# A two-block transformer kernel: the loads of shift and scale in eight 1 MB pieces, x's chunks ahead of the context's, and the low parts multiplied last

## The chip, the cores and the metric

The kernel runs on one core of one Trainium2 chip. The metric is the device time of one execution in microseconds (us). Three runs of the kernel before gave 1496.94 us in the median (1495.87 to 1498.08).

## The reference, cut to what matters

The program computes two transformer blocks on 512 tokens of 1024 features, all in float32. Only the very start of the first block is touched:

```
mod_l = split(silu(c) @ ada_w + ada_b, 6)          # ada_w: 1024 x 6144; shift, scale, gate, ...
mod_c = split(silu(c_ctx) @ ada_w + ada_b, 6)
h  = rmsnorm(x)   * norm1_g * (1 + scale)   + shift      # 512 tokens
hc = rmsnorm(ctx) * norm1_g * (1 + scale_c) + shift_c    # 256 tokens
z  = h @ w_in;   v = z[..., 1024:1536]
kvc = hc @ w_in[:, 512:1536]                             # its second half gives the context's v
```

Behind it stand the attention, the gating, the convolution and the feed-forward part of the first block, and the whole second block.

## The kernel before, in words

The program is written engine by engine: each engine has its own hand-written order of instructions, and semaphores tie them together. An engine's order is strict, so whatever waits holds up everything behind it on that engine. Features lie on the 128 partitions in eight chunks k = 0 to 7, and tokens along the free dimension.

**Products.** Every large product runs as three float32r matmuls: low times high, high times low, high times high. Of each weight tile ScalarE (ACT) makes the high part (`prepare`, L1092) and VectorE (DVE) the low part (`low`, L1547). Tiles arrive by SyncE (SP) in three raw slots, and three split tiles are kept.

**The beginning** runs until the first product of the tile called g0. It holds:

- The tiles of shift and scale, `ada_turned`: 16 tiles of 512 KB in seven slots, which are borrowed from buffers that are used later (`v_mid`, `q_loc`, `sg_out`, `sg_v`, `v_ctx`, `probs_more`). On PE, `modulation(i)` (L601) multiplies one with silu(c) and silu(c_ctx). Four tiles make a quarter. DVE copies the quarter's sums (L1635), PE adds up its parts (`selected`, L613), and DVE makes shift and gain for two chunks (`gains_of`, L1641 and L1644).
- The two norms: ACT squares (L1099), DVE adds (L1564), PE sums over partitions (`norm_sum`, L559), ACT takes the root (L1104), DVE its reciprocal (L1568), PE spreads it (`norm_spread`, L573), ACT copies it out (L1142 for x, L1154 for the context), and DVE multiplies (L1650, L1660).
- The chunks: ACT writes `exact` and then `h_hi` (`modulated`, L1119 and L1121), or `normed` and then `hc_hi` (`context`, L1128 and L1130). DVE subtracts for the low part (`modulated_lo`, L1655, and `context_lo`, L1665).
- The products for v: `own(k)` is 12 matmuls for chunk k of x (four token tiles into banks 0 to 3), `context(k)` is 6 for chunk k of the context (banks 4 and 5). Weight tile t holds chunks 2t and 2t + 1. So `own(4)` and `context(4)` need the third tile, and `own(6)` the fourth.
- Eight rows of `ada_rows` for the later gates: `early_rows` on DVE (L1573), in the same seven slots.

PE's order is: tile 0, sums of x's norm, tile 1, spread, tiles 2 and 3, selection 0, `own(0)`, tiles 4 to 7, selection 1, `own(1)`, `own(2)`, sums of the context's norm, tiles 8 to 11, `own(3)`, spread, selection 2, `context(0)`, `context(1)`, `own(4)`, tiles 12 to 15, `own(5)`, selection 3, `context(2)`, `context(3)`, `own(6)`, `context(4)`, `context(5)`, `own(7)`, `context(6)`, `context(7)`. Then g0 starts.

## Time and profile before

| | |
|---|---|
| median of three runs | 1496.94 us |
| the profiled execution | 1495.27 us |
| its span in the profile | 1494.0 us |
| PE busy | 1421.7 us, 95% of the span |
| DVE, ACT busy | 51%, 41% |
| start of the first product of g0 | 80.97 us |
| PE busy before 81.00 us | 57.89 us |

Times in the trace count from the span's start. A row of a timeline is a run of equal instructions: where it starts, how long it took, engine, line, operation, what it writes and reads, and, in brackets, how long the engine had been idle and what ended that. A row of the table by stage gives the busy time of each engine, the granted clock of PE as a share of full speed, the share of time in which the DMA engines were busy, and GB/s.

### The profile page before, as it was taken

To read this page: it belongs to the slowest core of one execution; us is meant where nothing else is said; L and a number is where in the kernel's file an instruction comes from. 1 tells how busy PE (TensorE), PEld (TensorE's weight loads), DVE (VectorE), ACT (ScalarE), POOL (GpSimd) and SP (SyncE) were. 2 spreads that over 40 slices of the span, in tenths; PEclk is the share of its full clock that TensorE was granted. 3 is DMA by queue.
4 is the path that set the end of the run, shared out by engine and by line. 5 is a ranking of instruction groups with operands and counts; after the bars stand their busy time and mean duration, and the time that the engine had idled before them with its cause. 6 is when DMAs were issued, how large, how long until landed. Compare 5 with 4: busy or idle time off the path is not lost.

```text
span 1494.0 us, 16901 instructions
## 1 busy us (share of the span) xinstructions
PE 1421.7 (95%) x6826; PEld 1147.6 (77%) x6826; DVE 766.4 (51%) x1005; ACT 617.6 (41%) x856; POOL 14.3 (1%) x20
## 2 busy tenths in 40 slices
PE   5899998989999999999999999999969999999997
PEld 3677776778888888887878877888857888888886
DVE  3568865555554443335327763443266566564224
ACT  4546776363333332223337643322334343343221
POOL 0000000000000000000000000000010000000000
PEclk9999999999999999999999999999959999999999
DMA  8653321303433233331321112233202323223331
GB/s 331 236 162 134 125 74 55 136 29 127 164 132 98 86 95 90 92 104 43 113 85 38 34 43 78 92 99 113 85 15 100 98 85 101 96 85 103 94 100 57
DMA packets 44317, 150.43 MB, mean 101 GB/s; under 512 B 4944, under 2 KB 7120, under 8 KB 44112
## 3 DMA queue, kind: packets, MB, share of 16 engines
q1 hardware_dynamic: 43360, 144.76, 29.3%
q0 software_dynamic: 880, 4.59, 1.0%
q8 instruction: 55, 0.90, 0.2%
q14 instruction: 22, 0.18, 0.0%
HBM read 146.45 MB, written 2.10 MB: 99 GB/s over the span
## 4 chain that ended last, share of the span: by engine, by line
PE 75%; DVE 3%; ACT 1%; issue 1%; POOL 0%; DVEq 0%; ACTq 0%
PE banks L514 23%; PE banks L516 23%; PE banks L515 23%; PE banks L932 1%; PE banks L933 1%; PE banks L559 1%; PE banks L927 1%; PE banks L966 1%; PE banks L924 1%; PE banks L963 1%; PE banks L573 0%; DVE y_buf L2117 0%; DVE x_res L2121 0%; DVE x_res L2056 0%; DVE y_buf L2052 0%
## 5 line engine op out<-in xcount | busy, mean ns | idle before, releaser
L514 PE MATMUL banks<-h_lo,w_hi 128*128 128x512 f32 x1184 | 475.1, 401 | 15.8 <-DVE cv_acc L1836 3.7
L1547 DVE TENSOR_TENSOR w_lo<-raw_w,w_hi 128x1024 fp32r<-128x1024 f32 (+2 forms) x229 | 266.2, 1164 | 402.6 <-ACT w_hi L1092 402.2
L516 PE MATMUL banks<-h_hi,w_hi 128*128 128x512 f32 x1184 | 469.8, 397 | 0.0
L515 PE MATMUL banks<-h_hi,w_lo 128*128 128x512 f32 x1184 | 469.7, 397 | 0.0
L1092 ACT ACTIVATE w_hi<-raw_w 128x1024 fp32r<-128x1024 f32 (+2 forms) x229 | 230.0, 1006 | 285.0 <-PE banks L516 263.3
L514 PEld LDWEIGHTS banks<-h_lo,w_hi 128*128 128x128 f32 x1184 | 224.8, 190 | 74.1 <-issue 20.5
L516 PEld LDWEIGHTS banks<-h_hi,w_hi 128*128 128x128 f32 x1184 | 224.5, 190 | 53.0
L515 PEld LDWEIGHTS banks<-h_hi,w_lo 128*128 128x128 f32 x1184 | 224.8, 190 | 50.1
L516 PE MATMUL banks<-a_hi,w_hi 128*128 128x512 f32 (+1 forms) x374 | 142.5, 381 | 0.0
L515 PE MATMUL banks<-a_hi,w_lo 128*128 128x512 f32 (+1 forms) x374 | 142.2, 380 | 0.0
L514 PE MATMUL banks<-a_lo,w_hi 128*128 128x512 f32 (+1 forms) x374 | 141.7, 379 | 0.0
L515 PEld LDWEIGHTS banks<-a_hi,w_lo 128*128 128x128 f32 x374 | 70.3, 188 | 14.8
L514 PEld LDWEIGHTS banks<-a_lo,w_hi 128*128 128x128 f32 x374 | 70.3, 188 | 14.5
L516 PEld LDWEIGHTS banks<-a_hi,w_hi 128*128 128x128 f32 x374 | 70.3, 188 | 13.7
L1616 DVE SCALAR_TENSOR_TENSOR exact<-banks,cols_sb,exact 128x510 f32<-128x510 f32 (+1 forms) x44 | 33.0, 750 | 53.5 <-ACT exact L1507 52.7
L1616 DVE SCALAR_TENSOR_TENSOR normed<-banks,cols_sb,normed 128x510 f32<-128x510 f32 (+1 forms) x66 | 49.2, 746 | 5.2 <-ACT normed L1507 2.9
L1507 ACT ACTIVATE exact<-banks,cols_sb 128x512 f32<-128x512 f32 x22 | 15.1, 688 | 83.1 <-PE banks L516 83.1
L1107 ACT ACTIVATE a_hi<-normed 128x512 fp32r<-128x512 f32 x44 | 27.8, 633 | 48.7 <-DVE normed L1894 32.0
L1610 DVE SCALAR_TENSOR_TENSOR cv_acc<-cv_in,cols_sb,cv_acc 128x512 f32<-128x512 f32 x60 | 45.0, 749 | 1.4
L1789 DVE SCALAR_TENSOR_TENSOR x_res<-banks,mod,x_res 128x512 f32<-128x512 f32 x22 | 16.2, 749 | 45.1 <-PE banks L516 45.1
L1350 ACT ACTIVATE normed<-normed 128x512 f32<-128x512 f32 x22 | 13.9, 632 | 53.0 <-DVE normed L1890 53.0
L514 PE MATMUL banks<-w_lo,h_hi 128*128 128x512 f32 x64 | 27.1, 423 | 4.7 <-DVE h_lo L1655 3.0
(291 smaller groups left out, 1549.1 us busy)
## 6 DMA issues: line engine op xcount, KB each, us to landing
raw_w<-in_w_ffn_up SPq DMA_DIRECT2D x44, 512.0 KB, 3.4
raw_w<-in_w_up SPq DMA_DIRECT2D x44, 512.0 KB, 3.4
raw_w<-in_ada_rows SPq DMA_DIRECT2D x24, 512.0 KB, 4.0
raw_w<-in_w_gates SPq DMA_DIRECT2D x16, 512.0 KB, 3.2
raw_w<-in_w_ffn_down SPq DMA_DIRECT2D x16, 448.0 KB, 3.3
raw_w<-in_w_down SPq DMA_DIRECT2D x16, 448.0 KB, 3.3
raw_w<-in_w_conv SPq DMA_DIRECT2D x12, 512.0 KB, 3.2
raw_w<-in_w_out SPq DMA_DIRECT2D x10, 512.0 KB, 3.3
```

The source lines that it names most:

```text
L514: e.matmul(dst, lhs_hi, rhs_lo, start=first, stop=False)
L515: e.matmul(dst, lhs_lo, rhs_hi, start=False, stop=False)
L516: return e.matmul(dst, lhs_hi, rhs_hi, start=False, stop=last)
L559: done = e.matmul(bank[b][:, t:t + 1], part[:, t * P:(t + 1) * P], ones[:, :], start=(first and t == 0), stop=(last and t == nt - 1), skip ...
L924: done = e.matmul(bank[0][:, DIAG[j]], keys, q2[part, c, j * P:(j + 1) * P], start=True, stop=True)
L1092: e.activation(w_hi[:, t % KEPT, 0:n], raw[:, i % RAW, 0:n], ACT.Copy).then_inc(s_hi, 1)
L1107: e.activation(dst, src, ACT.Copy).then_inc(done, 1)
L1507: e.activation(dst, bank[b[n]][:, :], ACT.Copy, scale=col("conv_ffn_w_2", w)).then_inc(s_up2_centre.sem, 1)
L1547: e.tensor_tensor(w_lo[:, s, 0:n], raw[:, i % RAW, 0:n], w_hi[:, s, 0:n].bitcast(F32), ALU.subtract).then_inc(s_lo, 1)
L1610: e.scalar_tensor_tensor(out=acc, in0=src, scalar=col("cv_w", i), in1=acc, op0=ALU.mult, op1=ALU.add).then_inc(s_tap_v, 1)
L1616: return e.scalar_tensor_tensor(out=y[:, shift:T], in0=src[:, 0:T - shift], scalar=w, in1=y[:, shift:T], op0=ALU.mult, op1=ALU.add)
L1789: e.scalar_tensor_tensor(out=x[:, o, :], in0=bank[b][:, :], scalar=mod[:, gate + o:gate + o + 1], in1=x[:, o, :], op0=ALU.mult, op1=ALU.ad ...
```

## The change

**Loads of shift and scale.** The same 8 MB come as 8 tiles of 1 MB in a buffer of their own with six slots (`EARLY_SLOTS`). `modulation(i)` now multiplies one such tile, with 8 matmuls where it had 4, and two tiles make a quarter. The eight rows of `ada_rows` come as four transfers of 1 MB in the slots 2, 3, 0 and 1. The buffer lies over `q_loc`, `v_mid`, `v_ctx`, `sg_out`, `sg_v`, `cv_in`, `sg_small` and `hc_hi`, so that their first writers wait: `hc_hi` for the sixth tile's product, the zeros beside `cv_in` (now on DVE behind the last early row) and the load of `sg_small` (now behind that of `v_mid`) for the eight rows.

**SP's queue.** All four transfers of x come first, then `consts` and `cols`, and tile 0 behind them.

**The norm of x.** DVE adds the eighth square too, so that PE sums once (4 instructions for 8). PE does that ahead of tile 0.

**Low parts last.** `values_of` multiplies the high part of a chunk with both parts of the weights, and only then waits for the chunk's low part. ACT writes the high part ahead of `exact` and `normed`.

**Orders.** PE takes `own(4)` ahead of `context(0)`, and `context(4)` ahead of `own(6)`. ACT and DVE follow in orders of their own.

```diff
-EARLY = 7
-ADA_TILES = 16
+EARLY_SLOTS = (0, 1, 2, 3, 4, 5, 0, 1, 2, 3, 0, 1)
+ADA_TILES = 8
...
-        n_one, n_ctx, n_two = NormSems(0), NormSems(0), NormSems(0, add=0, sum=KC)
+        n_one, n_ctx, n_two = NormSems(0, add=KC - 1), NormSems(0), NormSems(0, add=0, sum=KC)
...
+        def early_at(i):
+
+            slot = EARLY_SLOTS[i]
+            return early[:, slot, :, :], (s_early[slot], 16 * EARLY_SLOTS[:i + 1].count(slot))
...
-                e.wait_ge(*ready.at(k + 1))
+                e.wait_ge(*n_hi.at(k + 1))
                 for n, b in enumerate(banks):
                     if k == 0:
                         free(b)
                     tok = slice(n * P, (n + 1) * P)
-                    done = product(bank[b][:, :], src_hi[:, k, tok], src_lo[:, k, tok], hi[:, w], lo[:, w], k == 0, k == KC - 1)
...
+                    e.matmul(bank[b][:, :], src_hi[:, k, tok], lo[:, w], start=(k == 0), stop=False)
+                    e.matmul(bank[b][:, :], src_hi[:, k, tok], hi[:, w], start=False, stop=False)
+                e.wait_ge(*n_lo.at(k + 1))
+                for n, b in enumerate(banks):
+                    tok = slice(n * P, (n + 1) * P)
+                    done = e.matmul(bank[b][:, :], src_lo[:, k, tok], hi[:, w], start=False, stop=(k == KC - 1))
...
+            e.wait_ge(s_ones, 1)
+            e.wait_ge(*n_one.add.at(KC - 1))
+            sum_over_partitions(n_one.bank, exact[:, 0, :], TT, True, True).then_inc(n_one.sum.sem, 1)
             e.wait_ge(s_silu_c, 1)
             modulation(0)
-            norm_sum(n_one, exact[:, 0, :], squares[:, 0, :], TT)
-            modulation(1)
             norm_spread(n_one, TT)
             freed[n_one.bank] = (s_factor, 1)
+            modulation(1)
+            selected(0)
+            own(0)
             modulation(2)
             modulation(3)
-            selected(0)
-            own(0)
-            for i in range(4, 8):
-                modulation(i)
+            own(1)
             selected(1)
-            own(1)
             own(2)
             norm_sum(n_ctx, k_ctx[:, 0, :], squares[:, 0, 0:CTX], CT)
-            for i in range(8, 12):
-                modulation(i)
+            modulation(4)
             own(3)
+            modulation(5)
             norm_spread(n_ctx, CT)
             freed[n_ctx.bank] = (s_factor_ctx, 1)
             selected(2)
+            own(4)
             context(0)
+            own(5)
             context(1)
-            own(4)
-            for i in range(12, 16):
-                modulation(i)
-            own(5)
+            modulation(6)
+            modulation(7)
+            context(2)
             selected(3)
-            for k in range(2, KC):
-                context(k)
-                if k in (3, 5):
-                    own((k + 9) // 2)
+            context(3)
+            context(4)
+            own(6)
+            context(5)
+            own(7)
+            context(6)
+            context(7)
...
             e.dma_start(silu_c[:, :, :], io["c_cols"]).then_inc(s_c, 16)
-            load_x(0)
-            load_x(1)
+            for i in range(KC // 2):
+                load_x(i)
             e.dma_start(consts[:, :], io["consts"]).then_inc(s_consts, 16)
-            load_x(2)
-            load_x(3)
-            load_early(0, 2)
             e.dma_start(cols[:, :], io["cols"]).then_inc(s_cols, 16)
-            load_early(2, 4)
+            load_early(0, 1)
             load(0, 1)
-            load_early(4, 8)
+            load_early(1, 4)
             load(1, 2)
             e.dma_start(xc[:, :, :], io["ctx"]).then_inc(s_xc, 16)
-            load_early(8, 12)
+            load_early(4, 6)
+            load(2, 3)
+            load_early(6, ADA_TILES)
```

The order of the instructions shows what became of the calls. Three places matter. The line numbers of the change are those of its own file: L638, L639 and L643 are the three matmuls that are L514 to L516 before, L610 is a tile of shift and scale, L1111 the split of the weights, L1138 and L1140 `modulated`, L1148 and L1150 `context`.

PE, from the spread of the context's norm on (`hc_hi` is a chunk of the context, `h_hi` one of x). Before:

```order
L573 MATMUL banks<-consts_sb,rstd 128x128 x2
L613 MATMUL banks<-consts_sb,cv_scratch 128x4 x2
L514 MATMUL banks<-w_lo,hc_hi 128x512
L515 MATMUL banks<-w_hi,hc_lo 128x512
L516 MATMUL banks<-w_hi,hc_hi 128x512
L514 MATMUL banks<-w_lo,hc_hi 128x512
```

In the change:

```order
L579 MATMUL banks<-consts_sb,rstd 128x128 x2
L622 MATMUL banks<-consts_sb,cv_scratch 128x4 x2
L638 MATMUL banks<-w_lo,h_hi 128x512
L639 MATMUL banks<-w_hi,h_hi 128x512
L638 MATMUL banks<-w_lo,h_hi 128x512
L639 MATMUL banks<-w_hi,h_hi 128x512
```

Behind the selection PE now takes chunk 4 of x, which reads the third weight tile, where it took chunk 0 of the context, which reads the first.

ACT, around the split of the third weight tile (`w_hi<-raw_w`; `sg_square` is the factor of the context's norm, `v_loc` holds chunks 4 to 7 of x). Before:

```order
L1154 ACTIVATE sg_square<-banks 128x256
L1128 ACTIVATE normed<-xc,mods,gains 128x256
L1130 ACTIVATE hc_hi<-xc,mods,gains 128x256
L1128 ACTIVATE normed<-xc,mods,gains 128x256
L1130 ACTIVATE hc_hi<-xc,mods,gains 128x256
L1092 ACTIVATE w_hi<-raw_w 128x1024
```

In the change:

```order
L1123 ACTIVATE std<-banks,cols_sb 128x2
L1138 ACTIVATE h_hi<-v_loc,mods,gains 128x8x8x8
L1140 ACTIVATE exact<-v_loc,mods,gains 128x512
L1177 ACTIVATE sg_square<-banks 128x256
L1148 ACTIVATE hc_hi<-xc,mods,gains 128x256
L1150 ACTIVATE normed<-xc,mods,gains 128x256
L1111 ACTIVATE w_hi<-raw_w 128x1024
L1138 ACTIVATE h_hi<-v_loc,mods,gains 128x8x8x8
```

Chunk 4 of x has moved ahead of the norm's factor. The split stands behind chunk 0 of the context where it stood behind chunks 0 and 1, and chunk 4 of x, which is multiplied with this tile, stands ahead of it. On DVE the low part of the tile (`low(3)`) follows in both.

ACT, around the split of the fourth weight tile, from the silu of c's row on. Before:

```order
L1163 ACTIVATE silu_row<-silu_row 128x1024
L1119 ACTIVATE exact<-v_loc,mods,gains 128x512
L1121 ACTIVATE h_hi<-v_loc,mods,gains 128x8x8x8
L1092 ACTIVATE w_hi<-raw_w 128x1024
L1128 ACTIVATE normed<-xc,mods,gains 128x256
L1130 ACTIVATE hc_hi<-xc,mods,gains 128x256
L1128 ACTIVATE normed<-xc,mods,gains 128x256
L1130 ACTIVATE hc_hi<-xc,mods,gains 128x256
L1119 ACTIVATE exact<-v_loc,mods,gains 128x512
```

In the change:

```order
L1186 ACTIVATE silu_row<-silu_row 128x1024
L1148 ACTIVATE hc_hi<-xc,mods,gains 128x256
L1150 ACTIVATE normed<-xc,mods,gains 128x256
L1148 ACTIVATE hc_hi<-xc,mods,gains 128x256
L1150 ACTIVATE normed<-xc,mods,gains 128x256
L1138 ACTIVATE h_hi<-v_loc,mods,gains 128x8x8x8
L1140 ACTIVATE exact<-v_loc,mods,gains 128x512
L1111 ACTIVATE w_hi<-raw_w 128x1024
L1138 ACTIVATE h_hi<-v_loc,mods,gains 128x8x8x8
```

Two chunks of the context (`hc_hi`, `normed`) have moved ahead of chunk 6 of x and of the tile's split.

## Rows read from the trace of the kernel before

**Rows 1.** The page: engines' shares, and the chain that ended last.

```profile
PE 1421.7 (95%) x6826; PEld 1147.6 (77%) x6826; DVE 766.4 (51%) x1005; ACT 617.6 (41%) x856; POOL 14.3 (1%) x20
...
PE 75%; DVE 3%; ACT 1%; issue 1%; POOL 0%; DVEq 0%; ACTq 0%
```

**Rows 2.** PE's timeline up to the first products.

```profile
12.72 1.03 PE L601 MATMUL banks<-v_mid,silu_c 128*2 128x256 f32 x8 [12.72 <-DMA v_mid<-in_ada_turned]
...
15.42 1.85 PE L559 MATMUL banks<-ones,squares 128*128 128x1 f32 x8
...
18.16 2.08 PE L573 MATMUL banks<-consts_sb,rstd 128*128 128x128 f32 x8
...
22.69 0.58 PE L613 MATMUL banks<-consts_sb,cv_scratch 128*128 128x4 f32 x4 [0.64 <-DVE cv_scratch L1635]
26.29 0.77 PE L514 MATMUL banks<-w_lo,h_hi 128*128 128x512 f32 x1 [3.02 <-DVE h_lo L1655]
```

**Rows 3.** PE's timeline inside the first products.

```profile
26.86 0.63 PE L515 MATMUL banks<-w_hi,h_lo 128*128 128x512 f32 x1
27.28 0.63 PE L516 MATMUL banks<-w_hi,h_hi 128*128 128x512 f32 x1
...
29.63 0.39 PE L516 MATMUL banks<-w_hi,h_hi 128*128 128x512 f32 x1
29.86 0.39 PE L514 MATMUL banks<-w_lo,h_hi 128*128 128x512 f32 x1
```

**Rows 4.** PE's timeline: own(2), sums, selections, then restarts, then g0.

```profile
36.75 0.47 PE L514 MATMUL banks<-w_lo,h_hi 128*128 128x512 f32 x1
...
41.15 0.58 PE L559 MATMUL banks<-ones,k_ctx 128*128 128x1 f32 x4 [1.36 <-DVE k_ctx L1564]
...
48.86 0.51 PE L613 MATMUL banks<-consts_sb,cv_scratch 128*128 128x4 f32 x4
52.07 0.47 PE L514 MATMUL banks<-w_lo,hc_hi 128*128 128x512 f32 x1 [2.71 <-issue]
...
64.11 0.50 PE L613 MATMUL banks<-consts_sb,cv_scratch 128*128 128x4 f32 x4
...
69.03 0.50 PE L514 MATMUL banks<-w_lo,h_hi 128*128 128x512 f32 x1 [1.52 <-DVE w_lo L1547]
...
80.97 0.40 PE L514 MATMUL banks<-h_lo,w_hi 128*128 128x512 f32 x1
```

**Rows 5.** By stage: engines busy, granted clock, DMA's share, GB/s.

```profile
12.70:26.20 13.50, 9.90 (x60) 6.43 (x60) 4.32 (x10) 5.68 (x9) 0.00 (x0) 0.99 1.03 419
...
49.40:52.10 2.70, 0.03 (x1) 0.06 (x1) 1.42 (x5) 2.21 (x6) 0.00 (x0) 1.00 1.02 410
53.10:56.40 3.30, 3.30 (x10) 2.55 (x9) 3.00 (x5) 3.30 (x6) 0.00 (x0) 0.52 0.09 34
```

**Rows 6.** ACT's timeline: x's squares, a chunk of x, a weight split, the context's.

```profile
10.05 1.15 ACT L1099 ACTIVATE squares<-x_res 128x512 f32<-128x512 f32 x2 [2.29 <-DMA x_res<-in_x]
...
65.16 0.82 ACT L1119 ACTIVATE exact<-v_loc,mods,gains 128x512 f32<-128x512 f32 x1 [5.04 <-issue]
...
66.59 1.04 ACT L1092 ACTIVATE w_hi<-raw_w 128x1024 fp32r<-128x1024 f32 x1
67.54 0.58 ACT L1128 ACTIVATE normed<-xc,mods,gains 128x256 f32<-128x256 f32 x1
68.03 0.59 ACT L1130 ACTIVATE hc_hi<-xc,mods,gains 128x256 fp32r<-128x256 f32 x1
```

**Rows 7.** DVE's timeline: the norm's adds, the gains, low parts.

```profile
10.71 2.29 DVE L1564 TENSOR_TENSOR exact<-exact,squares 128x512 f32<-128x512 f32 x3 [2.00 <-ACT squares L1099]
...
64.91 0.16 DVE L1644 SCALAR_TENSOR_TENSOR gains<-mods,cols_sb 128x4 f32<-128x4 f32 x1
...
67.15 0.69 DVE L1655 TENSOR_TENSOR h_lo<-exact,h_hi 128x512 fp32r<-128x512 f32 x1
67.75 1.22 DVE L1547 TENSOR_TENSOR w_lo<-raw_w,w_hi 128x1024 fp32r<-128x1024 f32 x1
```

More of the change, by code:

```diff
@@ L297, in two_blocks @@
                 group_factor = sb(mixer, "group_factor", [P, CC * TT * 2])
+                with ExitStack() as beginning:
+                    early = sb(beginning, "early", [P, 6, 2, SLOT])
+                q_loc = sb(mixer, "q_loc", [P, AC, T])
+                v_mid = sb(mixer, "v_mid", [P, CBLK - 1, ATT])
+                v_ctx = sb(mixer, "v_ctx", [P, CT, ATT])
+                sg_out = sb(mixer, "sg_out", [P, SC, T])
+                sg_v = sb(mixer, "sg_v", [P, TT, SG])
+                cv_in = sb(mixer, "cv_in", [P, CC, T + 2 * PAD])
+                sg_small = sb(mixer, "sg_small_sb", [P, SC * P + 2 * SG + 4 * P])
+                hc_hi = sb(mixer, "hc_hi", [P, KC, CTX], F32R)
+                hc_lo = sb(mixer, "hc_lo", [P, KC, CTX], F32R)
                 with ExitStack() as context:
@@ L381, in two_blocks @@
         s_bias = [semaphore(f"in_bias{i}") for i in range(2)]
-        s_early = [semaphore(f"in_early{i}") for i in range(EARLY)]
+        s_early = [semaphore(f"in_early{i}") for i in range(6)]
         s_x = [semaphore(f"in_x{i}") for i in range(KC // 2)]
@@ L593, in modulation @@
             def modulation(i):
-                quarter, m = i // 4, i % 4
+                quarter = i // 2
                 b = ADA_BANKS[quarter]
-                if m == 0:
+                tiles, there = early_at(i)
+                if i % 2 == 0:
                     free(b)
-                e.wait_ge(s_early[i % EARLY], 16 * (i // EARLY + 1))
-                for part in range(4):
-                    done = e.matmul(bank[b][32 * part:32 * part + 2, 0:2 * P], silu_c[:, 2 * m + part // 2, :],
-                                    early[i % EARLY][:, part * 2 * P:(part + 1) * 2 * P], start=(m == 0), stop=(m == 3))
+                e.wait_ge(*there)
+                for half in range(2):
+                    m = 2 * (i % 2) + half
+                    for part in range(4):
+                        done = e.matmul(bank[b][32 * part:32 * part + 2, 0:2 * P], silu_c[:, 2 * m + part // 2, :],
+                                        tiles[:, half, part * 2 * P:(part + 1) * 2 * P], start=(m == 0), stop=(m == 3))
                 done.then_inc(s_modulation, 1)
-                if m == 3:
+                if i % 2:
                     freed[b] = (s_ada_sums, quarter + 1)
@@ L616, in selected, with values_of @@
                 freed[select_bank] = (s_mods, quarter + 1)
[L618 removed]
+            def values_of(k, banks, src, n_hi, n_lo):
+                src_hi, src_lo = src
                 t = W["v"] + k // 2
@@ L1579, in early_rows @@
                 for _ in range(count):
-                    i = ADA_TILES + rows_done
-                    e.wait_ge(s_early[i % EARLY], 16 * (i // EARLY + 1))
-                    row(early[i % EARLY])
+                    tiles, there = early_at(ADA_TILES + rows_done // 2)
+                    e.wait_ge(*there)
+                    row(tiles[:, rows_done % 2, :])
             def rows(before):
@@ L1668, in vector_program @@
                 e.memset(bank[b][:, 0:2 * P], 0.0).then_inc(s_cleared, 1)
-            for k in range(1, KC - 1):
+            for k in range(1, KC):
                 add(n_one, k, exact[:, 0, :], squares[:, (k - 1) % 2, :])
             reciprocal_root(n_one, TT)
+            low(1)
             normed_x(0)
+            modulation(0)
             normed_x(1)
-            modulation(0)
             gains_of(0)
-            low(1)
             modulated_lo(0)
@@ L1707, in vector_program @@
             context_lo(3)
-            early_rows(1)
             normed_context(4)
             normed_context(5)
+            context_lo(4)
+            context_lo(5)
             modulated_lo(6)
             low(4)
-            early_rows(1)
-            context_lo(4)
-            context_lo(5)
-            modulated_lo(7)
-            early_rows(1)
             normed_context(6)
             normed_context(7)
-            early_rows(1)
-            low(W["g0"] + 1)
+            modulated_lo(7)
+            early_rows(2)
             context_lo(6)
             context_lo(7)
+            low(W["g0"] + 1)
+            early_rows(1)
             low(W["g0"] + 2)
-            early_rows(EARLY_ROWS - 4)
+            early_rows(EARLY_ROWS - 3)
+            e.wait_ge(s_row, EARLY_ROWS)
+            for s in (slice(0, PAD), slice(PAD + T, T + 2 * PAD)):
+                e.memset(cv_in[:, :, s], 0.0).then_inc(s_pads, 1)
             def softmax(i):
```

94 lines of the change are left out of this document (44 added, 50 removed).

## The prediction

> **What bounds the kernel now.** I read the page first: PE is busy for 95% of the span and holds 75% of the chain that ended last, far ahead of any other engine [rows 1]. So a microsecond won or lost on PE in the beginning arrives at the end undiminished, as long as PE finds no gap behind g0 to hide it in. Next I read PE's timeline of the beginning, which is all that the change touches. It shows where PE stands still: 12.7 us until tile 0, 3.0 us before `own(0)`, 1.4 us before the sums of the context's norm, 2.7 us before `context(0)`, 1.5 us before `own(6)`, which waits for the low part of the fourth weight tile [rows 2, 4]. g0 starts at 80.97 us, and that start is the number to forecast. The table by stage shows that DMA is saturated early on, at 419 GB/s with a share of 1.03 [rows 5], but of PE's waits only the first one ends on a DMA. The others end on chains through ACT and DVE. So the question is how these chains are ordered.
>
> Prices for PE. A matmul of 512 columns starts every 0.42 us at the lower level of the clock (1.2 GHz) and every 0.23 us at the upper (2.4 GHz) [rows 3]. So a chunk of x (12) costs 5.1 or 2.8 us, a chunk of the context (6) 2.5 or 1.4 us. A tile of 512 KB costs 0.97 us at the lower level (its row's 1.03 less the overlap) [rows 2], about half of that at the upper. The eight sums of 1.85 us and the spread of 2.08 us [rows 2] fell at the lower level too: four sums later took 0.58 us [rows 4].
>
> **Step 1, the lead.** x's third transfer was there at 10.05 us [rows 6]. The 322 KB of constants no longer stand ahead of it, which at 419 GB/s [rows 5] is 0.8 us. The last three adds ended at 13.0 us (10.71 + 2.29) [rows 7]; now they end at 12.2, and one add more (0.6) makes 12.8. One group of sums follows where two were, to 14.7 us. Tile 0 is 1 MB. The queue's bytes up to its end are 3.7 MB where they were 3.0 MB at 12.72 us, so it lands at about 14.5 us, hidden under the sums. It runs to 16.6 (2 x 0.97). The root's table load now stands behind the wait for the sums and is hidden under tile 0. The spread ends at 18.7, ACT's copy and DVE's product for chunk 0 at 20.0. Tile 1 runs 18.7 to 20.6, and DVE's copy lets the selection start at 21.1, where it was 22.69 [rows 2]. From the start of a selection to the end of the gains it takes 0.96 us (64.11 to 65.07) [rows 4, 7], and `h_hi` is written first now and takes 0.8 us, as a chunk's first write does [rows 6]. `own(0)` starts at 23.05 instead of 26.29 us: **a lead of 3.2 us**. The low part is ready long before PE wants it.
>
> **Step 2, it shrinks.** `own(0)` ends at 27.2 (7 matmuls at the lower level, 5 at the upper). Tiles 2 and 3 (1.75) and `own(1)` (2.8) lead to 31.8, and only there does selection 1 follow. Its gains come at 32.7. The low part of the second weight tile stands behind them on DVE (1.2) [rows 7], so `own(2)` starts at 33.9, where it was 36.75 [rows 4]: a lead of 2.85. It ends at 36.7. PE then waits for the context's norm. ACT's squares begin at 34.2 behind chunk 2. Of the six adds (0.5 us each) three stand behind the low part of chunk 3, which waits for ACT's `exact` of chunk 3, itself put between the squares: the last add ends at 39.5. The sums start there and not at 41.15 [rows 4]: a lead of 1.65, and PE has stood still for 2.8 us.
>
> **Step 3, to selection 2.** Sums, tile 4, `own(3)`, tile 5 and the spread take 6.1 us at the upper level, 9.4 us where half of it falls at the lower. Selection 2 starts between 45.6 and 48.9; before it was 48.86 [rows 4].
>
> **Step 4, the third weight tile.** Here the lead is lost. PE's next work is `own(4)`, which needs this tile's low part. ACT splits it behind chunk 4 of x, the norm's factor and `context(0)`, and DVE behind the low parts of both. From the start of the selection: gains 0.96, chunk 4 on ACT 1.45, the factor 0.4 beside the low part of chunk 4, the product of context and factor 0.4, `context(0)` 1.0, the high part of the weights 1.05, its low part 1.2, and some 0.3 between engines: 6.8 us, where `context(0)` came 3.2 us behind the selection (48.86 to 52.07) [rows 4, 6, 7]. So PE restarts between 52.4 and 55.7. I take 54.5, since the idle 2.8 us of step 2 speak for the lower clock: before, after 2.71 us without work, a stage followed at 0.52 [rows 4, 5]. Work ahead of 52.07 before and of this restart is otherwise equal (`own(0)` to `own(3)`), so 2.4 us are lost here.
>
> **Step 5, the fourth weight tile.** From 54.5: `own(4)`, `context(0)`, `own(5)`, `context(1)` are 36 matmuls, 8 of them at the lower level, 9.9 us; tiles 6 and 7 take 1.8, `context(2)` 1.4. Selection 3 starts at 67.6; before, 64.11. The chain to `own(6)`: gains 0.96, low part of `context(3)` 0.4, product 0.4, `context(4)` and `context(5)` at 4 x 0.49 (67.54 to 68.03), chunk 6 1.43 (65.16 to 66.59), the split 1.05 and 1.2 [rows 4, 6, 7]: 7.6 us, where it was 4.9 (64.11 to 69.03). `own(6)` starts at 75.2. PE has done `context(3)` and `context(4)` by 71.4 and stands still for 3.8 us. Behind it `own(6)`, `context(5)`, `own(7)`, `context(6)`, `context(7)` take 9.8 us, up to 1.6 more when the clock has fallen: I take 1.2.
>
> The clock of steps 4 and 5 is where a page bears on this change. The stage behind the pause at 49.4 to 52.1 us was granted 0.52 [rows 5]. The Trainium skill says the same (TensorE: Matmul & The Clock Gate, the section on HAM oscillation): waits between bursts of matmuls bring the clock down, and each burst then starts cold. It speaks against an order that turns two short waits into two long ones. By that rule the sum below stands at its upper half; without it at the lower bound.
>
> **The sum.** g0 starts at 75.2 + 9.8 + 1.2 = 86.2 us instead of 80.97: 5.2 us later. The rest costs nothing: the zeros beside `cv_in` and `sg_small`'s load come some 80 us ahead of their use; the early rows (eight of 1.2 us on DVE) end at about 89 us, and the weights of k0 behind them at 93 us, ahead of PE, which wants them at 97. The profiled execution would take 1495.27 + 5.2 = 1500.5 us; its median was 1.67 us above it, so 1502.1 us. Bounds: with step 3 at its low end and no clock lost behind `own(6)`, g0 starts at 82.9 (+1.9, 1498.9 us); at the high end 87.8 (+6.8, 1503.7 us).
>
> **The rivals.**
>
> *The clock holds.* PE keeps the upper level through steps 2 and 3, and behind `own(6)`: +1.9 us, 1498.9 us. For it: the 1.5 us before `own(6)` cost no clock. Against it: the new pauses are longer. A measurement of this kernel tells about 0.2% (3 us) from no change, so most of this case reads as the same.
>
> *The lead arrives.* The mechanism: PE gets the third weight tile as early as `own(4)`'s own chunk, so that the lead is not lost in step 4. That takes its low part by 48.8 us. All of the 3.2 us then reach g0: 1493.7 us, faster. For it: the tile's bytes are in SBUF long before, and ACT is idle between the root and the gains. Against it: both engines' orders put the split behind `context(0)`, and an order isn't passed over. Transfers of 512 KB ran at 419 GB/s [rows 5], so larger ones can't help either. The Trainium skill (DMA: Bandwidth & Descriptors, Bandwidth) advises transfers of 1 MiB or more, with 341 GB/s measured for 1 MB. The trace is above that at half the size, and no term moves.
>
> *The rows are late.* The last pair of early rows is asked for behind tile 7's product at 66 us. Should it land over 5 us later than I think, ACT is held at the context's values, the weights of k0 miss PE, and 2 us come on top: 1504.1 us.
>
> **How the numbers follow.** My forecast 0.60, all of it slower. The clock holds 0.20: 0.15 the same, 0.05 slower. The rows are late 0.08, slower. The lead arrives 0.12: 0.10 faster, 0.02 the same. That makes 0.10 faster, 0.17 the same, 0.73 slower. The likeliest case gives 1502.1 us. The range reaches from 1496.5 us, below the case of the held clock, to 1505.5 us, above the bound with late rows, and leaves out little but the faster case.
>
> **What would show it.** Right: `own(0)` near 23 us; a pause of some 6 us before `own(4)` that ends on a `w_lo`; one of 3 to 4 us before `own(6)`, also ending on `w_lo`; g0 near 86 us. Wrong: `own(4)` starting before 52 us, or g0 before 81 us; or a difference that arises behind g0.

## The result, and the profile after

The change is slower: 1504.03 us in the median of four runs (1503.41 to 1507.15), against 1497.51 us for the kernel before beside it (four runs, 1495.87 to 1498.32). The ratio, taken from the means, is 1.0049, its 95% interval 1.0032 to 1.0067.

| | before | after | forecast |
|---|---|---|---|
| median, us | 1497.51 | 1504.03 | 1502.1 |
| the profiled execution, us | 1495.27 | 1503.41 | 1500.5 |
| its span, us | 1494.0 | 1502.1 | |
| start of `own(0)`, us | 26.29 | 21.55 | 23.05 |
| restart behind selection 2, us | 52.07 | 54.91 | 54.5 |
| `own(6)`, us | 69.03 | 75.73 | 75.2 |
| first product of g0, us | 80.97 | 86.92 | 86.2 |

The page of the kernel after, its engines' shares and the chain that ended last (beside [rows 1]): the bound is the same.

```profile
PE 1424.9 (95%) x6818; PEld 1150.3 (77%) x6818; DVE 767.3 (51%) x1006; ACT 617.9 (41%) x856; POOL 14.2 (1%) x20
...
PE 74%; DVE 3%; ACT 1%; issue 1%; POOL 0%; DVEq 0%; ACTq 0%
```

PE's timeline of the kernel after (beside [rows 2, 4]). L565 is a norm's sums, L610 a tile of shift and scale, L622 a selection, L638 the first matmul of a chunk.

```profile
12.09 1.84 PE L565 MATMUL banks<-ones,exact 128*128 128x1 f32 x8 [12.09 <-DVE exact L1587]
13.86 1.89 PE L610 MATMUL banks<-early,silu_c 128*2 128x256 f32 x16
15.82 1.79 PE L579 MATMUL banks<-consts_sb,rstd 128*128 128x128 f32 x8
17.54 1.05 PE L610 MATMUL banks<-early,silu_c 128*2 128x256 f32 x16
19.45 0.58 PE L622 MATMUL banks<-consts_sb,cv_scratch 128*128 128x4 f32 x4 [0.86 <-DVE cv_scratch L1656]
21.55 0.77 PE L638 MATMUL banks<-w_lo,h_hi 128*128 128x512 f32 x1 [1.52 <-ACT h_hi L1138]
...
31.88 0.50 PE L622 MATMUL banks<-consts_sb,cv_scratch 128*128 128x4 f32 x4
34.04 0.65 PE L638 MATMUL banks<-w_lo,h_hi 128*128 128x512 f32 x1 [1.66 <-DVE w_lo L1570]
...
39.65 0.58 PE L565 MATMUL banks<-ones,k_ctx 128*128 128x1 f32 x4 [1.00 <-DVE k_ctx L1587]
...
47.77 0.58 PE L622 MATMUL banks<-consts_sb,cv_scratch 128*128 128x4 f32 x4
54.91 0.79 PE L638 MATMUL banks<-w_lo,h_hi 128*128 128x512 f32 x1 [6.57 <-DVE w_lo L1570]
...
68.29 0.50 PE L622 MATMUL banks<-consts_sb,cv_scratch 128*128 128x4 f32 x4
...
75.73 0.80 PE L638 MATMUL banks<-w_lo,h_hi 128*128 128x512 f32 x1 [3.37 <-DVE w_lo L1570]
...
86.92 0.39 PE L520 MATMUL banks<-h_lo,w_hi 128*128 128x512 f32 x1
```

The lead is there at `own(0)` and it is 4.7 us. It has shrunk to 2.7 us at `own(2)` (36.75 before) and to 1.1 us at selection 2 (48.86 before). Then PE stands still for 6.57 us and for 3.37 us. Both pauses end on `w_lo`, the low part of a weight tile. The lag at g0 is 5.95 us.

What `own(4)` waits for at 54.91 us is plain from ACT's timeline of the kernel after,

```profile
48.90 0.81 ACT L1138 ACTIVATE h_hi<-v_loc,mods,gains 128x512 fp32r<-128x512 f32 x1 [7.92 <-DVE gains L1665]
49.62 0.80 ACT L1140 ACTIVATE exact<-v_loc,mods,gains 128x512 f32<-128x512 f32 x1
50.32 0.36 ACT L1177 ACTIVATE sg_square<-banks 128x256 f32<-128x256 f32 x1
51.56 0.60 ACT L1148 ACTIVATE hc_hi<-xc,mods,gains 128x256 fp32r<-128x256 f32 x1 [0.88 <-issue]
52.07 0.58 ACT L1150 ACTIVATE normed<-xc,mods,gains 128x256 f32<-128x256 f32 x1
52.56 1.04 ACT L1111 ACTIVATE w_hi<-raw_w 128x1024 fp32r<-128x1024 f32 x1
```

and from DVE's:

```profile
48.65 0.16 DVE L1665 SCALAR_TENSOR_TENSOR gains<-mods,cols_sb 128x4 f32<-128x4 f32 x1
...
53.63 1.23 DVE L1570 TENSOR_TENSOR w_lo<-raw_w,w_hi 128x1024 fp32r<-128x1024 f32 x1
```

The high part of chunk 4, which is multiplied with this tile, is written from 48.90 us on. ACT had been idle for 7.92 us before that. The split of the tile (L1111) starts at 52.56 us only, and its low part ends at 54.86 us, just ahead of PE's restart. It is the chain of step 4.

The table by stage for the kernel after (columns as in [rows 5]):

```profile
34.00:39.00 5.00, 4.61 (x12) 3.32 (x12) 3.34 (x7) 4.23 (x10) 0.00 (x0) 0.66 1.01 410
...
55.00:58.00 3.00, 3.00 (x7) 2.38 (x8) 2.67 (x6) 2.98 (x8) 0.00 (x0) 0.50 0.01 3
...
284.00:288.00 4.00, 4.00 (x15) 3.29 (x14) 0.00 (x0) 1.03 (x1) 0.00 (x0) 0.65 0.45 180
```

and for the kernel before:

```profile
34.00:39.00 5.00, 4.89 (x22) 3.67 (x21) 3.46 (x8) 4.36 (x9) 0.67 (x1) 1.00 0.99 402
...
278.00:282.00 4.00, 4.00 (x30) 3.03 (x29) 1.35 (x2) 1.54 (x2) 0.00 (x0) 1.00 0.31 123
```

Behind the long pause the granted clock is 0.50, the lower of the two levels. In the first 20 us this column can't be used to tell the levels: it says 1.00 for this stretch of the kernel after,

```profile
12.00:20.00 8.00, 6.97 (x52) 4.62 (x52) 3.03 (x5) 3.09 (x4) 0.00 (x0) 1.00 1.02 427
```

although tile 0 takes 1.89 us in it and tile 1, equal work, 1.05 us (and 0.99 in [rows 5], where the prediction reads the lower level too). There the level is read from the times of equal work. The last row of each table belongs to a second difference, which the forecast doesn't have. Matched product by product, PE's lag stays between 4.9 and 6 us from g0 until some 250 us (80.97 against 86.92, 251.61 against 257.31), and is 8.1 us from 280.5 us on (280.52 against 288.63). Of these 2.4 us, 1.0 arises at once behind 251.61 (253.01 against 259.72), where the granted clock is 1.00 before and 0.59 after, and 1.4 behind a pause that both kernels have. In the timeline of the kernel before,

```profile
276.39 1.24 PE L733 MATMUL banks<-consts_sb,normed 128*128 128x128 f32 x8 [3.12 <-ACT normed L1213]
```

and of the kernel after:

```profile
283.04 1.71 PE L752 MATMUL banks<-consts_sb,normed 128*128 128x128 f32 x8 [3.05 <-ACT normed L1236]
```

The same work was granted 1.00 behind it before, and 0.65 after. Nothing of the change is near. The two spans differ by 8.1 us, the medians by 6.5 us.

### The profile page after: what moved, and what is told of

The parts are those of the page before. It is cut to its first block, busy times and chain, and to the rows that moved or that the text cites. A ratio compares the mean times of both kernels' runs of the same rounds, so it can differ in the third digit from the quotient of the medians.

```text
span 1502.1 us, 16877 instructions
## 1 busy us (share of the span) xinstructions
PE 1424.9 (95%) x6818; PEld 1150.3 (77%) x6818; DVE 767.3 (51%) x1006; ACT 617.9 (41%) x856; POOL 14.2 (1%) x20
## 4 chain that ended last, share of the span: by engine, by line
PE 74%; DVE 3%; ACT 1%; issue 1%; POOL 0%; DVEq 0%; ACTq 0%
PE banks L520 23%; PE banks L522 23%; PE banks L521 23%; PE banks L951 1%; PE banks L952 1%; PE banks L946 1%; PE banks L985 1%; PE banks L565 1%; PE banks L943 1%; PE banks L982 1%; PE banks L579 0%; DVE y_buf L2141 0%; DVE x_res L2145 0%; DVE x_res L2080 0%; DVE y_buf L2076 0%
## 5 line engine op out<-in xcount | busy, mean ns | idle before, releaser
L1111 ACT ACTIVATE w_hi<-raw_w 128x1024 fp32r<-128x1024 f32 (+2 forms) x229 | 230.1, 1006 | 289.5 <-PE banks L522 264.8
L521 PEld LDWEIGHTS banks<-a_hi,w_lo 128*128 128x128 f32 x374 | 70.3, 188 | 14.5
L520 PEld LDWEIGHTS banks<-a_lo,w_hi 128*128 128x128 f32 x374 | 70.3, 188 | 13.8
L1918 DVE TENSOR_TENSOR normed<-banks,normed 128x512 f32<-128x512 f32 x22 | 15.2, 692 | 30.7 <-PE banks L522 24.4
```

The lines of the kernel that those rows point to most:

```text
L520: e.matmul(dst, lhs_hi, rhs_lo, start=first, stop=False)
L521: e.matmul(dst, lhs_lo, rhs_hi, start=False, stop=False)
L1111: e.activation(w_hi[:, t % KEPT, 0:n], raw[:, i % RAW, 0:n], ACT.Copy).then_inc(s_hi, 1)
L1918: e.tensor_tensor(y, bank[(b + 1) % 6][:, :], y, ALU.mult).then_inc(s_up_act, 1)
```

## The experiments

The theory: the whole loss stems from two places in ACT's and DVE's orders, where the splits of the third and fourth weight tiles stand behind chunks that PE doesn't yet need. The rivals: the size of the transfers, the low parts multiplied last, PE's order alone, or an effect of the new start. In the diffs, the first hunk is ACT's order and the second DVE's, unless said otherwise. Traces of kernels with the same beginning differ by some tenths up to a microsecond in their first starts, so I read distances from the selection ahead more than absolute times. From selection 2 to g0 it is 32.1 us in the kernel before (48.86 to 80.97) and 39.2 us in the change (47.77 to 86.92).

**1. The third tile's split early.** In the change, the split moves into ACT's idle stretch and its low part into DVE's.

```diff
             root(n_ctx, CT)
+            prepare(3)
             modulated(4)
...
             context(0)
-            prepare(3)
...
             reciprocal_root(n_ctx, CT)
+            low(3)
             modulation(2)
...
             normed_context(1)
-            low(3)
```

> The change, with the split of the third weight tile (high part on ACT, low part on DVE) moved ahead of chunk 4 of x, into the time in which both engines wait for the selection. Theory (the order of the splits cost the time): PE restarts at own(4) when h_hi of chunk 4 is there, near 49.8 us instead of 54.9, everything behind moves by 5 us, g0 starts near 82 us instead of 86.9, and the run takes 5 us less than the change, about 1499. Rival (the 1 MB loads, or the low parts multiplied last, cost it): the restart of own(4) moves, but g0 stays within 1 us of 86.9. Rival (the clock is what counts): g0 comes more than 5 us earlier, since the shorter pause keeps the upper level.

Measured: 1498.78 us in the median of 10 runs, ratio to the kernel before 1.0017 (1.0002 to 1.0032). The split on ACT and its low part on DVE, then PE's timeline, `own(4)` and `own(6)`:

```profile
40.85 1.05 ACT L1111 ACTIVATE w_hi<-raw_w 128x1024 fp32r<-128x1024 f32 x1
...
41.93 1.23 DVE L1570 TENSOR_TENSOR w_lo<-raw_w,w_hi 128x1024 fp32r<-128x1024 f32 x1 [0.78 <-ACT w_hi L1111]
...
50.98 0.47 PE L638 MATMUL banks<-w_lo,h_hi 128*128 128x512 f32 x1 [1.51 <-ACT h_hi L1138]
...
70.33 0.76 PE L638 MATMUL banks<-w_lo,h_hi 128*128 128x512 f32 x1 [3.37 <-DVE w_lo L1570]
```

`own(4)` waits for its own chunk now, 2.1 us behind the selection (48.88) where it was 7.1 us. The second pause is untouched, to the hundredth. g0 starts at 81.78 us, 5.1 us earlier than in the change. So this one place holds 5 of the 6 us, and the clock is in it: the wait is 5.0 us shorter, and from `own(4)` to selection 3 it is 1.5 us less (50.98 to 62.89, against 54.91 to 68.29), with a granted clock of 1.00 from 53 to 58 us instead of 0.50; selection 2 came 1.1 us later than in the change, which takes part of it back. From selection 2 to g0 it is 32.9 us.

**2. Both splits early.** In addition:

```diff
             e.activation(silu_row[:, :], silu_row[:, :], ACT.Silu).then_inc(s_silu_row, 1)
+            prepare(4)
             context(4)
...
             modulated(6)
-            prepare(4)
             modulated(7)
...
             normed_x(7)
+            low(4)
             modulation(3)
...
             modulated_lo(6)
-            low(4)
```

> As third_split_early, and the split of the fourth weight tile moved too: on ACT behind the silu of c's row, on DVE ahead of the copy of the last quarter's sums. Theory: own(6) then waits for its own chunk only, 2 to 3 us less; g0 near 78 to 79 us, the run about 1495 to 1496, just faster than the kernel before. Rival (another chain takes over at once): g0 not before 81 us.

Measured: 1494.97 us (10 runs), ratio 0.9991 (0.9981 to 1.0002). `own(6)` and g0 on PE:

```profile
69.05 0.47 PE L638 MATMUL banks<-w_lo,h_hi 128*128 128x512 f32 x1 [0.55 <-ACT h_hi L1138]
...
78.91 0.39 PE L520 MATMUL banks<-h_lo,w_hi 128*128 128x512 f32 x1
```

g0 is 8.0 us earlier than in the change and 2.1 us earlier than before. From selection 2 (49.28) to g0 it is 29.6 us. With two instructions moved on each of two engines the change's loss is gone. It isn't a measurable gain over the kernel before: the interval holds 1.

**3. The fourth tile's split early, alone.** The diff of run 2 on the change, without that of run 1.

> The change with the split of the fourth weight tile alone moved ahead. Theory: own(4) still restarts near 54.9 us; own(6) starts near 72.9 instead of 75.7 us, g0 near 84 us, the run 3 us less than the change, about 1501. Rival (only the first of the two pauses counts, since PE is fed late in any case): own(6) and g0 as in the change.

Measured: 1499.84 us (6 runs), ratio 1.003 (1.0017 to 1.0042). `own(4)` keeps its pause of 6.57 us on `w_lo`. `own(6)`:

```profile
75.52 0.47 PE L638 MATMUL banks<-w_lo,h_hi 128*128 128x512 f32 x1 [0.55 <-ACT h_hi L1138]
```

Its pause has shrunk by 2.8 us, as in run 2. The absolute times missed (72.9 and 84 expected, 75.52 and 85.38 found): selection 2 came at 49.50 us, 1.7 us later than in the change, since PE got the lower level of the clock at another place. g0 moved by 1.5 us only. By g0 the two places give 5.1 and 1.5 us alone and 8.0 together. From selection 2 to g0 they add up: 39.2 us in the change, 6.3 less with the third split early, 3.3 less here (35.9), and 9.5 less with both.

**4. Halved transfers.** Each 1 MB transfer of the change is issued as two of 512 KB:

```diff
-                        e.dma_start(tiles, io["ada_turned"][i, :, :, :]).then_inc(there, 16)
+                        for half in range(2):
+                            e.dma_start(tiles[:, half, :], io["ada_turned"][i, :, half, :]).then_inc(there, 16)
```

and so for the rows.

> The change with each 1 MB transfer of shift, scale and early rows issued as two of 512 KB into the same slot. Theory (the size of the transfers decides nothing here): x's chain and own(0) at 21.5 us as in the change, every start on PE within 0.5 us, g0 within 0.7 us of 86.9. Rival (1 MB pieces land sooner and bring the lead): own(0) more than 0.7 us later.

Measured: 1504.88 us in one run. `own(0)` at 21.88 us, `own(2)` at 33.29, `own(4)` at 55.74 behind the same 6.57 us on `w_lo`, `own(6)` at 76.81 behind the same 3.37 us. No wait of PE grew or shrank on a transfer. g0 came at 88.13 us, 1.2 us later than in the change 0.5 more than I allowed; from selection 2 to g0 it is 0.4 us more (39.5). The distance from `own(0)` to `own(2)` was even 1.1 us shorter, that from `own(2)` to `own(4)` 1.6 us longer, nearly all of it between the sums (38.92) and selection 2 (48.59), where more of PE's rows have the times of the lower level. The size of the transfers isn't the cause.

**5. The low parts in the middle.** The change's orders and loads, with the products of `values_of` grouped as before:

```diff
-                    e.matmul(bank[b][:, :], src_hi[:, k, tok], lo[:, w], start=(k == 0), stop=False)
-                    e.matmul(bank[b][:, :], src_hi[:, k, tok], hi[:, w], start=False, stop=False)
-                e.wait_ge(*n_lo.at(k + 1))
-                for n, b in enumerate(banks):
-                    tok = slice(n * P, (n + 1) * P)
-                    done = e.matmul(bank[b][:, :], src_lo[:, k, tok], hi[:, w], start=False, stop=(k == KC - 1))
+                    if n == 0:
+                        e.wait_ge(*n_lo.at(k + 1))
+                    done = product(bank[b][:, :], src_hi[:, k, tok], src_lo[:, k, tok], hi[:, w], lo[:, w], k == 0, k == KC - 1)
```

> The change with the three matmuls of each product in v in the old order and grouping, so that every chunk waits for its low part first. Theory (the low parts last are worth the time between the high and the low part of chunk 0, 0.7 for exact and 0.7 on DVE): own(0) waits for DVE and starts 1.3 us later after its selection (from selection 0 to own(0) 3.4 us instead of 2.1), the pause between selection 2 and own(4) stays 7.1 us, g0 about 1.5 us later than in the change. Rival (the low parts are hidden anyway): no start moves by more than 0.5 us.

Measured: 1505.9 us in one run. `own(0)` and `own(2)`:

```profile
23.57 0.76 PE L520 MATMUL banks<-w_lo,h_hi 128*128 128x512 f32 x1 [2.96 <-DVE h_lo L1673]
...
37.12 0.47 PE L520 MATMUL banks<-w_lo,h_hi 128*128 128x512 f32 x1 [2.95 <-DVE h_lo L1673]
```

`own(0)` stands 3.5 us behind its selection instead of 2.1. g0 is 1.4 us later than in the change (88.30), as forecast. The low parts last are a gain, not the loss.

**6. The context before x on PE.** PE's order alone is turned back to one chunk of the context first:

```diff
-            own(4)
             context(0)
-            own(5)
+            own(4)
             context(1)
+            own(5)
             modulation(6)
```

> The change with PE's order alone put back at the first pause: context(0), own(4), context(1), own(5). Theory (own(4) waits for the third weight tile, context(0) needs the first): PE restarts 2.5 to 2.8 us earlier, from selection 2 to the restart 4.4 us instead of 7.1; own(4) then waits little or not at all; g0 1.4 to 2.5 us earlier than in the change. Rival (the wait is for the context's norm as much as for the tile): the restart comes less than 1 us earlier.

Measured: 1502.13 us in one run. The restart:

```profile
53.58 0.76 PE L638 MATMUL banks<-w_lo,hc_hi 128*128 128x512 f32 x1 [3.92 <-issue]
```

It comes 4.5 us behind the selection (49.08) instead of 7.1, since the context's chunk reads the first weight tile and waits for its own high part only (written from 52.88 us on). g0 is 1.3 us earlier (85.63), just short of the 1.4 to 2.5 us expected; from selection 2 to g0 it is 2.6 us less (36.6). So PE's order alone gives back a fifth of the loss by g0, and a little over a third of it (2.6 of 7.0 us) counted from selection 2. These aren't shares beside those of runs 1 to 3: both ways shorten the same wait.

**7. x first, in the kernel before.**

```diff
-            load_x(0)
-            load_x(1)
+            for i in range(KC // 2):
+                load_x(i)
             e.dma_start(consts[:, :], io["consts"]).then_inc(s_consts, 16)
-            load_x(2)
-            load_x(3)
```

> The kernel before with the constants loaded behind all of x, nothing else. Theory (PE's sums stand behind tile 0 of shift and scale, so x earlier brings nothing by itself): the squares of chunks 4 to 7 start 0.8 us earlier, the sums and own(0) where they were (15.4 and 26.3 us) within 0.4 us, g0 as before. Rival (x's load bounds the start): own(0) 0.8 us earlier or more.

Measured: 1496.06 us in one run, with 1495.68 us for the kernel before (9 runs). The third pair of squares starts at 8.18 us instead of 10.05. The first tile:

```profile
11.64 1.03 PE L601 MATMUL banks<-v_mid,silu_c 128*2 128x256 f32 x8 [11.64 <-DMA v_mid<-in_ada_turned]
```

It landed 1.1 us earlier although as many bytes stand ahead of it, if in another order. Run 12, with the loads of before as they are, shows that 0.6 us of such a difference comes without any change (12.13 us). The sums started 1.1 us earlier with it (14.33 instead of 15.42 for the second group), where none was expected, `own(0)` is 0.7 us earlier (25.62; within 0.4 was expected), g0 0.5 us (80.44). Alone, this part is worth nothing that can be told apart here.

**8. Rearranged.** The change's loads, start and products, with new orders on all three engines. PE, behind tile 1:

```diff
-            own(1)
             selected(1)
-            own(2)
+            own(1)
             norm_sum(n_ctx, k_ctx[:, 0, :], squares[:, 0, 0:CTX], CT)
+            own(2)
             modulation(4)
-            own(3)
             modulation(5)
             norm_spread(n_ctx, CT)
...
             selected(2)
+            own(3)
             own(4)
             context(0)
-            own(5)
-            context(1)
             modulation(6)
             modulation(7)
-            context(2)
+            context(1)
             selected(3)
+            own(5)
+            context(2)
             context(3)
-            context(4)
             own(6)
+            context(4)
             context(5)
```

Behind selections 1 to 3 and behind the sums of the context's norm, PE now has a chunk that is ready. On ACT the context's squares come before chunks 2 and 3, `prepare(3)` right behind the root, and `prepare(4)` behind chunk 6. On DVE `low(2)` and `low(3)` come as soon as their high parts are there, `low(4)` behind chunk 6, and the adds of the context's norm come ahead of the low parts of chunks 2 and 3.

> The change with its loads and products as they are, and new orders on PE, ACT and DVE: the splits of the second, third and fourth weight tiles as soon as they can be, the context's squares in ACT's idle time behind chunk 1, tiles 4 and 5 and the spread ahead of own(3), selections 1, 2 and 3 directly behind the copy of their sums with a chunk's products between selection and use. Theory (the order was the fault, not the loads): PE never stands still for over 1.5 us behind own(0), g0 starts between 66 and 71 us, the run takes 1482 to 1488 us, 0.6% to 0.9% less than the kernel before. Rival (ACT and DVE have too much to do by then and set the pace, each with some 40 us of work ahead of g0): g0 not before 76 us.

Measured: 1482.9 us in the median of 5 runs (1481.47 to 1485.25), the kernel before 1495.68 (9 runs), ratio 0.9913 (0.9897 to 0.9928). PE's timeline, `own(0)` and g0:

```profile
22.48 0.47 PE L638 MATMUL banks<-w_lo,h_hi 128*128 128x512 f32 x1 [1.52 <-ACT h_hi L1138]
...
67.22 0.39 PE L520 MATMUL banks<-h_lo,w_hi 128*128 128x512 f32 x1
```

The table by stage, between the two:

```profile
22.40:67.20 44.80, 44.11 (x264) 32.71 (x265) 31.88 (x62) 31.57 (x52) 1.23 (x2) 0.96 0.81 320
```

PE is busy for 44.11 of 44.80 us at a granted clock of 0.96. g0 is 19.7 us earlier than in the change and 13.8 us earlier than before. This beats both kernels. What each of the moves gives by itself wasn't measured.

**9. Rearranged, with the start of before.** Constants ahead of x's third transfer, tile 0 (1 MB still) ahead of `cols` and, on PE, ahead of the sums, and the sums in two groups.

```diff
-            e.wait_ge(s_ones, 1)
-            e.wait_ge(*n_one.add.at(KC - 1))
-            sum_over_partitions(n_one.bank, exact[:, 0, :], TT, True, True).then_inc(n_one.sum.sem, 1)
             e.wait_ge(s_silu_c, 1)
             modulation(0)
+            norm_sum(n_one, exact[:, 0, :], squares[:, 0, :], TT)
             norm_spread(n_one, TT)
...
-            for i in range(KC // 2):
-                load_x(i)
+            load_x(0)
+            load_x(1)
             e.dma_start(consts[:, :], io["consts"]).then_inc(s_consts, 16)
-            e.dma_start(cols[:, :], io["cols"]).then_inc(s_cols, 16)
+            load_x(2)
+            load_x(3)
             load_early(0, 1)
+            e.dma_start(cols[:, :], io["cols"]).then_inc(s_cols, 16)
```

> The rearranged order of the previous run (1482.9 us, own(0) at 22.48, g0 at 67.22), with the beginning of the kernel before: constants ahead of x's third transfer, tile 0 ahead of the columns, tile 0's product ahead of the sums, the sums in two groups. If the beginning itself is a gain that the split weights' place on ACT and DVE had hidden, own(0) comes 2 to 3 us later (about 25) and g0 at 69 to 70.5, with a time near 1485.5. Rival: the lead is absorbed by the row of the context or by the loads even in this order; then own(0) comes late but g0 stays at 67 to 68 and the time within 1 us of 1482.9.

Measured: 1486.98 us (5 runs, 1484.55 to 1490.88), ratio 0.9941 (0.9919 to 0.9963). PE's timeline:

```profile
13.68 1.89 PE L610 MATMUL banks<-early,silu_c 128*2 128x256 f32 x16 [13.68 <-DMA early<-in_ada_turned]
15.49 1.87 PE L565 MATMUL banks<-ones,exact 128*128 128x1 f32 x8
17.22 1.85 PE L565 MATMUL banks<-ones,squares 128*128 128x1 f32 x8
...
26.67 0.76 PE L638 MATMUL banks<-w_lo,h_hi 128*128 128x512 f32 x1 [1.52 <-ACT h_hi L1136]
```

`own(0)` is 4.2 us later than in run 8, and g0 5.0 us (72.18). In the change, a lead of 4.7 us at `own(0)` ended as a lag of 6; here all of the 4.2 us arrives. It isn't the worth of the new start against that of before, where tile 0 has 512 KB and is there at 12.72 us: `own(0)` of the kernel before, at 26.29 us, is 3.8 us behind that of run 8. I had expected 2 to 3 us: with a tile of 1 MB ahead of the sums, these start at 15.5 us rather than at 12.1, and there are two groups of them. The intervals of the two ratios still touch, so the size in the median (some 4 us) is less certain than the trace's.

**10. Rearranged, with halved transfers.** The diff of run 4 on run 8.

> The rearranged order with each 1 MB transfer issued as two of 512 KB. Theory: the size of the transfer is worth nothing here; own(0) within 0.5 us of 22.48, g0 within 0.8 us of 67.22 and the time within 1.5 us of 1482.9. Rival: with PE no longer waiting for split weights the loads are the next to be late and the size matters; then PE's waits for tiles grow and g0 moves by more than 1.5 us.

Measured: 1483.88 us (4 runs), ratio 0.9909 (0.9883 to 0.9934). `own(0)` is at 23.43 us and g0 at 68.15, 0.95 and 0.93 us later, both more than allowed (0.5 and 0.8). The delay is there at the first sums already (13.06 against 12.12): ACT got x's second transfer at 7.59 us, behind a wait of 1.28 us that run 8 doesn't have, and that transfer stands ahead of every halved one in the queue. From there on the starts keep their distances. Even with PE hardly ever waiting, the size of the transfers is worth nothing that shows.

**11. Rearranged, low parts in the middle.** The diff of run 5 on run 8.

> The rearranged order with the low parts multiplied in the order of the kernel before (the products with a split activation's low part ahead of the last group). Theory: the first product of the two own modulations whose low part is late waits 1.3 to 1.4 us more, so own(0) comes at 23.8 to 23.9 and g0 1.3 to 2.5 us later than 67.22, the time about 1484.5. Rival: PE has work queued that makes up for it, g0 within 0.6 us of 67.22 and the time within 1 us of 1482.9.

Measured: 1484.63 us (4 runs), ratio 0.9926 (0.9899 to 0.9954). On PE:

```profile
22.89 0.77 PE L520 MATMUL banks<-w_lo,h_hi 128*128 128x512 f32 x1 [2.95 <-DVE h_lo L1672]
```

This is 3.5 us behind the selection (19.36), where run 8 has 2.1 us. `own(0)` is only 0.4 us later than in run 8 (1.3 to 1.4 were expected), since the selection came 1.0 us earlier, behind a tile 1 that ran at the upper level (1.05 us instead of 1.89). g0 comes 1.2 us later (68.42; 1.3 to 2.5 were expected). The medians can't tell 1.2 us.

**12. The kernel before, its fourth tile's split early.**

```diff
-            modulated(6)
             prepare(4)
+            modulated(6)
             context(4)
...
             normed_x(6)
+            low(4)
             modulation(3)
...
             modulated_lo(6)
-            low(4)
```

> The kernel before with the fourth weight chunk's split moved early on ACT and DVE and nothing else. Theory: own(6), which before ran at 69.03 behind the split weight, is released by the low part of its own activation instead, at about 67.9, and g0 comes about 1.1 us earlier than 80.97, at 79.9. Rival: the split weight isn't what held it; own(6) stays at 69.0 and g0 at 81.0.

Measured: 1494.97 us in one run, the kernel before beside it 1496.18 (8 runs). `own(6)`:

```profile
67.77 0.47 PE L514 MATMUL banks<-w_lo,h_hi 128*128 128x512 f32 x1 [0.48 <-DVE h_lo L1655]
```

It is released by its own chunk's low part, 1.3 us earlier than at 69.03, of which 0.2 us is there at `own(0)` already. g0 is 0.8 us earlier (80.17), since the next pause, before `context(6)`, grew from 0.42 to 0.92 us. So the fourth split held PE before too, only for less.

## Why the prediction was right

**Step 1, the lead: right in kind, too small.** Forecast 3.2 us, measured 4.7 (21.55 against 26.29). Two terms were mis-sized. x's last squares waited for no transfer any more: they ran from 8.05 us on, each behind a slot that DVE frees, so that the adds ended at 11.94 us (7.27 + 4.67) instead of 12.8. And tile 0 was there when the sums were done (13.86; I had it land at 14.5 us), and tile 1 at the upper level took 1.05 us, not 1.9. (From selection 0 to `own(0)` the terms named add up to 1.76 us, and the forecast has 1.95; measured 2.10.) The table load did hide under tile 0.

**Step 2: right in the chains, and in the times by luck.** `own(2)` at 34.04 (forecast 33.9), the sums at 39.65 (39.5), both by the chains named. But `own(0)` had started 1.5 us earlier than forecast. It lost that again because PE stayed at the lower level for all of `own(0)`, which took 5.4 us (21.55 to 26.94) and not 4.1, and into tiles 2 and 3 (2.0 us, not 1.75). The two misses cancel out. The pause ahead of the sums was 1.0 us instead of 2.8, because `own(2)` itself ran at a granted clock of 0.66; in runs 1 to 3 it was 2.56 or 2.57 us.

**Step 3: right here, though the bound was too narrow.** Selection 2 at 47.77 us, between 45.6 and 48.9. In runs 1 to 4 and 6, whose orders are the same up to there, it came at 48.59 to 49.50 us, 9.6 to 9.7 us behind the sums where the forecast had 9.4 at most.

**Step 4: right, and the main term.** The chain from the selection to the third tile's low part was forecast at 6.8 us and took 7.1; ACT's 0.88 us of idle time behind the factor is what I had as 0.4. PE restarted at 54.91 (54.5). Run 1 took this chain away and 5 us went with it. Run 6 showed that PE's order by itself shortens this wait by 2.6 us, of which 1.3 us reached g0.

**Step 5: right.** Selection 3 at 68.29 (67.6), the chain behind it 7.4 us (7.6 in the forecast, whose terms add up to 7.4), the pause 3.37 us (3.8), `own(6)` at 75.73 (75.2), its tail 11.2 us (11.0). g0 was 0.7 us later than forecast. Run 3 shrank this pause by 2.8 us with the split moved and nothing else.

**"The rest costs nothing": wrong by 2 us in this profile.** The prediction named a difference that arises behind g0 as a sign of being wrong, and there is one: the lag grew from 5.95 us at g0 to 8.1 between 250 and 290 us, in stages with equal work, where the granted clock was 0.59 and 0.65 against 1.00 of before. The late rows, my third rival, aren't the cause: up to 250 us the lag nowhere exceeds the 5.95 us of g0, and rows that held up the weights of k0 would have shown as a step near 97 us. The other runs speak for scatter. From g0 to the end of the span the change took 1415.2 us. Run 3, with the same program from there on, took 1412.8, runs 1, 2, 4, 5 and 6 took 1415.2 to 1416.3, and the rearranged kernels 1413.4 to 1418.0; the three kernels with before's program took 1413.0 to 1414.3. So one trace can't tell 2 us there, though a part of it that lasts isn't excluded. The medians lie 6.5 us apart, so it isn't a full 8 us, and runs 1 to 3 have ratios in the order of their g0 (g0 at +0.8, -2.1 and +4.4 us against before; ratios 1.0017, 0.9991 and 1.003). The median lies 1.9 us above the forecast. That the case of the late rows had 1504.1 us is a coincidence: its mechanism didn't occur (the early rows ended at 89.6 us, forecast 89).

**The rivals.** That the clock holds fell: the stage behind the long pause was granted 0.50, and `own(0)` to `own(2)` too had the lower level in places. That the lead arrives was rightly refused here, and the condition named for it, the third tile's low part as early as `own(4)`'s own chunk, is what run 1 made true; still nothing of the lead arrived (g0 0.8 us later than before), because the fourth tile's split stood behind it in the same manner. With that moved too (run 2), 2.1 us of a lead of 3.7 at `own(0)` arrived. Runs 8 and 9 show the start's lead arriving once neither PE nor the two helpers have anything in the wrong place. That larger transfers can't help was right in both orders (runs 4 and 10).

## What to carry to other kernels

A lead at the first product can be worth nothing, as here, until each later wait has been followed in the helpers' own orders: ask of every long instruction on ACT or DVE (here the split of a weight tile) when its input is there, and put it into the idle stretch ahead of the chain that the next product needs, not behind it. If PE's order is changed so that other operands are wanted first, the orders of the engines that make them have to follow. And on the bounding engine keep one ready chunk behind each short product whose result has to travel around (a selection, a sum, a spread): run 8 has the change's own instructions in another order, and is 12.8 us faster than the kernel before.

## What the runs showed of the hardware

A pause of the same length ahead of the same work was followed by different clocks: 3.12 us, then a granted clock of 1.00 in the kernel before (278 to 282 us); 3.05 us, then 0.65 in the kernel after (284 to 288 us). It happened behind a pause of 0.88 us too, which both kernels have ahead of 250.38 and 255.53 us: 1.00 in the one, 0.59 in the other. In runs 1 to 3, whose orders are the change's up to there, `own(0)` started at the upper level (its first matmul took 0.47 us), while in the change it ran at the lower one (0.77 us). Up to selection 2 these kernels differed by 1.1 to 1.7 us in this way (47.77 us in the change, 48.88 to 49.50 in runs 1 to 3), most of it between the sums and the selection (8.1 us in the change, 9.6 to 9.7 in the runs), and a forecast of a few microseconds can't be better than that.

The arrival of the first tile, counted from the span's start, isn't fixed either: PE took it at 12.72 us in the kernel before and at 12.13 in run 12, whose loads are those of before. In run 7, with as many bytes ahead of it in another order, it was 11.64.
